# Modulation rows in units of 1024 by 512, in pairs, with a pair in each stage end

## What is computed

```python
def adaln(cond, w, b):                       # w is (2048, 6*2048) per layer
    m = jax.nn.silu(cond) @ w + b            # shift, scale, gate, twice
    return [m.reshape(n, 6, 1, D_MODEL)[:, j] for j in range(6)]

for l in range(2):
    sh1, sc1, g1, sh2, sc2, g2 = adaln(cond, w_ada[l], b_ada[l])
    h = rmsnorm(x, norm_g[l, 0]) * (1 + sc1) + sh1
    y = mixer(l, h)                          # 0: neighbourhood attention, 1: gated linear attention
    x = x + g1 * rmsnorm(y, norm_g[l, 1])
    h = rmsnorm(x, norm_g[l, 2]) * (1 + sc2) + sh2
    x = x + g2 * rmsnorm(square(relu(h @ w1[l])) @ w2[l], norm_g[l, 3])
```

## Time and profile before

| | us |
|---|---|
| runs | 2574.95, 2575.25, 2572.07 |
| median | 2574.95 |
| profiled execution, its time | 2574.7 |
| profiled execution, its span | 2572.9 |
| PE busy | 2508.4 (97%) |
| DVE busy | 1366.2 (53%) |
| ACT busy | 1052.7 (41%) |
| DMA, mean | 247 GB/s |

### The profile page before, as it was taken

The page is one execution under the profiler, slowest core; times in us unless marked ns, Lnnn a source line. Parts: engine busy times, 40 slices in busy tenths (PEclk is TensorE's granted clock), DMA queues, the critical chain, the costliest instruction groups (busy, mean ns, idle before and its releaser), DMA issues.

```text
span 2572.9 us, 37557 instructions
## 1 busy us (share of the span) xinstructions
PE 2508.4 (97%) x14850; PEld 2027.9 (79%) x14850; DVE 1366.2 (53%) x1496; ACT 1052.7 (41%) x1148; POOL 114.6 (4%) x164
## 2 busy tenths in 40 slices
PE   6899999989999999999999999999899999999998
PEld 3578888778878878878777877897787888888887
DVE  2244445475545536536555454564765464564665
ACT  3223344363334333423353365583533333343342
POOL 0020000000000000000000032200000000000000
PEclk8999999999999999999999999999999999999999
DMA  9988988958878878878787754559588555555554
GB/s 361 360 271 287 291 287 285 348 174 277 294 252 272 281 243 279 278 259 264 265 300 266 251 179 159 166 169 334 179 260 288 183 187 205 166 193 197 184 196 175
DMA packets 497463, 634.54 MB, mean 247 GB/s; under 512 B 12128, under 2 KB 378512, under 8 KB 496080
## 3 DMA queue, kind: packets, MB, share of 16 engines
q1 hardware_dynamic: 488672, 608.46, 70.9%
q0 software_dynamic: 6352, 23.31, 2.6%
q10 hardware_dynamic: 2336, 1.31, 0.2%
HBM read 623.90 MB, written 9.13 MB: 246 GB/s over the span
## 4 chain that ended last, share of the span: by engine, by line
PE 80%; DMA 10%; DVE 5%; ACT 3%; issue 1%; SPq 0%; POOL 0%; ACTq 0%; DVEq 0%
PE PS L1256 23%; PE PS L1257 12%; PE PS L1324 10%; PE PS L1326 10%; PE PS L1325 10%; PE PS L1283 4%; DVE WLO L1816 3%; ACT WHI L1560 2%; DMA RAW<-in_w_qkvg_gla 2%; DMA RAW<-in_w_o_na 2%; DMA RAW<-in_w_mlp 2%; DMA RAW<-in_w_o_gla 2%; PE PS L1265 2%; PE PS L1267 1%; PE PS L1266 1%; DMA SCR<-in_w_ada 1%
## 5 line engine op out<-in xcount | busy, mean ns | idle before, releaser
L1816 DVE TENSOR_TENSOR WLO<-RAW,WHI 128x2048 fp32r<-128x2048 f32 x384 | 878.8, 2300 | 767.0 <-ACT WHI L1560 762.2
L1560 ACT ACTIVATE WHI<-RAW 128x2048 fp32r<-128x2048 f32 x384 | 731.7, 1915 | 729.7 <-DMA RAW<-in_w_mlp 484.8
L1256 PE MATMUL PS<-HM,WHI 128*128 128x512 f32 x2560 | 913.8, 401 | 7.3 <-DVE SCR L2053 3.5
L1257 PE MATMUL PS<-HM,WLO 128*128 128x256 f32 x2560 | 718.5, 281 | 0.0
L1256 PEld LDWEIGHTS PS<-HM,WHI 128*128 128x128 f32 x2560 | 482.2, 188 | 139.3 <-issue 18.4
L1257 PEld LDWEIGHTS PS<-HM,WLO 128*128 128x128 f32 x2560 | 484.6, 189 | 0.2
L1324 PE MATMUL PS<-WHI,HID 128*128 128x512 f32 x1152 | 453.9, 394 | 6.0 <-DVE WLO L1816 6.0
L1325 PE MATMUL PS<-WLO,HID 128*128 128x512 f32 x1152 | 449.6, 390 | 0.0
L1326 PE MATMUL PS<-WHI,HID 128*128 128x512 f32 x1152 | 449.2, 390 | 0.0
L1324 PEld LDWEIGHTS PS<-WHI,HID 128*128 128x128 f32 x1152 | 216.8, 188 | 63.6 <-issue 19.3
L1326 PEld LDWEIGHTS PS<-WHI,HID 128*128 128x128 f32 x1152 | 216.8, 188 | 45.9
(11 more groups left out here) (238 smaller groups left out, 1882.4 us busy)
## 6 DMA issues: line engine op xcount, KB each, us to landing
RAW<-in_w_mlp SPq DMA_DIRECT2D x256, 1024.0 KB, 5.8
ADW<-in_w_ada SPq DMA_DIRECT2D x176, 1024.0 KB, 8.5
RAW<-in_w_qkv_na SPq DMA_DIRECT2D x48, 1024.0 KB, 6.8
RAW<-in_w_qkvg_gla SPq DMA_DIRECT2D x32, 1024.0 KB, 6.4
SCR<-in_w_ada SPq DMA_DIRECT2D x16, 1024.0 KB, 11.3
RAW<-in_w_o_na SPq DMA_DIRECT2D x16, 1024.0 KB, 7.1
RAW<-in_w_qkvg_gla SPq DMA_DIRECT2D x32, 512.0 KB, 4.8
RAW<-in_w_o_gla SPq DMA_DIRECT2D x16, 1024.0 KB, 7.0
```

The lines of the kernel that those rows point to most:

```text
L1256: mm(bank[:, 0:2 * T2], hi[:, k, cols], act[:, kc, 0:2 * T2], start=first, stop=False)
L1257: return mm(bank[:, 0:T2], lo[:, k, cols], act[:, kc, 0:T2], start=False, stop=last)
L1560: actv(WHI[:, 2 * s + u, 0:n], RAW[:, u, 0:n], ACT.Copy).then_inc(hi_done, 1)
L1816: tt(WLO[:, 2 * s + u, 0:n], RAW[:, u, 0:n], WHI[:, 2 * s + u, 0:n].bitcast(f32), ALU.subtract).then_inc(lo_done, 1)
```

## The change

- A unit is now 1024 rows by 512 columns, also 2 MB; its two halves are 512 rows by 512 columns. Two units (`odd` 0 and 1) accumulate in one bank, and give the same two rows of 256 as before. PE does 8 products of 512 columns per unit instead of 16 of 256. `row_ready` is waited for once in a pair.
- ACT copies and stores a pair as two halves of 256 columns, after both units. In attention this is at odd r, both halves in a row, each copy followed by its two stores, ahead of the split.
- There are 80 units as before. MLP 0 has 10 a group instead of 9, and the four stretches after it fewer.
- Each stage end has a pair instead of a single unit: the first unit ahead of the last turning of stream 0, the second behind it. ACT copies both after all four quarters of modulation.
- On SP the pair's loads take both places of the last output slab.

```diff
-        A_MLP0 = 5 * D // UC + 1
-        GU = 2 * NB + 1
-        A_QKV1 = A_MLP0 + HID_GROUPS * GU + 1
-        A_WO1 = A_QKV1 + NB + 2
-        A_MLP1 = A_WO1 + NB + 1
-        LU = 2 * NB - 1
-        A_END = A_MLP1 + LU
-        BETWEEN = {0: A_MLP0 - 1, 1: A_QKV1 - 1, 2: A_MLP1 - 1}
+        A_MLP0 = 5 * D // UC + 2
+        GU = 2 * NB + 2
+        A_QKV1 = A_MLP0 + HID_GROUPS * GU + 2
+        A_WO1 = A_QKV1 + NB
+        A_MLP1 = A_WO1 + NB
+        A_END = A_MLP1 + NB
+        BETWEEN = {0: A_MLP0 - 2, 1: A_QKV1 - 2, 2: A_MLP1 - 2}
...
-        PLAN_WO0, PLAN_WO, PLAN_V = ((0, 1), (2, 3), (4, 5), ()), ((0,), (1,), (2, 3), ()), ((0, 1), (2, 3), (4,), (5,))
-        PLAN_MLP = {GU: ((0,), (1,), (2, 3), (4,)), LU: ((0,), (1,), (2,), ())}
+        PLAN_WO0, PLAN_WO, PLAN_V = ((0, 1), (2, 3), (4, 5), ()), ((0,), (1,), (), ()), ((0,), (1,), (2,), (3,))
+        PLAN_MLP = {GU: ((0, 1), (2, 3), (4, 5), ()), NB: ((), (), (), ())}
...
                 if r == LAST:
-                    ada_row(A_QKV0 + r)
+                    row_half(A_QKV0 + r - 1, 0)
+                    row_half(A_QKV0 + r - 1, 1, MROW_NA)
                 for x in heads:
                     turned_keys(x)
-                if r < LAST:
-                    ada_row(A_QKV0 + r, r == 0)
+                if r < LAST and r % 2:
+                    row_half(A_QKV0 + r - 1, 0, first=r == 1)
+                    row_half(A_QKV0 + r - 1, 1, MROW_NA, first=r == 1)
                 split_hi(m, s, UNIT, (0,))
-                store_row(A_QKV0 + r)
...
-            def load_ada(a, layer, col):
+            def load_ada(a, layer, col, odd):
                 for u in range(2):
                     sp.wait_ge(ada0_used if u == 0 else ada_done, a + 1)
-                    src = w_ada[layer, u * UNIT_ROWS:(u + 1) * UNIT_ROWS, ds(col, UC)] \
-                        .rearrange("(c p) n -> p c n", p=P)
-                    sp.dma_start(ADW[:, u, :].rearrange("p (c n) -> p c n", c=UKC), src).then_inc(ada_in[u], 16)
+                    row = UNIT_ROWS * odd + YC * u
+                    src = w_ada[layer, row:row + YC, ds(col, AC)].rearrange("(c p) n -> p c n", p=P)
+                    sp.dma_start(ADW[:, u, :].rearrange("p (c n) -> p c n", c=4), src).then_inc(ada_in[u], 16)
...
             def with_between(plan, n):
-                return plan[n] + ((max(map(max, filter(None, plan))) + 1,) if n == YN - 1 else ())
+                last = max(map(max, filter(None, plan)))
+                return plan[n] + ((last + 1, last + 2) if n == YN - 1 else ())
...
-            def ada_rows(a, bank=ROWB):
-                pe.wait_ge(row_ready, a)
+            def ada_rows(a, odd, bank=ROWB):
+                if not odd:
+                    pe.wait_ge(row_ready, a)
                 for u in range(2):
                     pe.wait_ge(ada_in[u], ada_loads(a))
-                    w = ADW[:, u, :].rearrange("p (c n) -> p c n", c=UKC)
-                    for r in range(2):
-                        for j in range(4):
-                            k = 4 * r + j
-                            end = mm(bank[32 * j:32 * j + 32, 0:UC], CS[:, UKC * u + k, :], w[:, k, :],
-                                     start=(u == 0 and r == 0), stop=(u == 1 and r == 1))
+                    w = ADW[:, u, :].rearrange("p (c n) -> p c n", c=4)
+                    for j in range(4):
+                        end = mm(bank[32 * j:32 * j + 32, 0:AC], CS[:, UKC * odd + 4 * u + j, :], w[:, j, :],
+                                 start=(not odd and u == 0), stop=(odd == 1 and u == 1))
                     end.then_inc(ada0_used if u == 0 else ada_done, 1)
...
             def turn_rest(f, m0):
+                first = BETWEEN[f - 1]
+                pe.wait_ge(bank_free, evacuated(m0, YN - 2, 1))
+                ada_rows(first, 0, BETWEEN_ROWB)
                 turn_stream(f, 0, range(2, 4))
-                pe.wait_ge(bank_free, evacuated(m0, YN - 2, 1))
-                ada_rows(BETWEEN[f - 1], BETWEEN_ROWB)
+                ada_rows(first + 1, 1, BETWEEN_ROWB)
                 turn_stream(f, 1, range(4))
-                pe.wait_ge(row_ready, BETWEEN[f - 1] + 1)
+                pe.wait_ge(row_ready, first + 2)
...
-                    ada_row(BETWEEN[f], False, BETWEEN_ROWB)
                     modulate(f + 1, shift, 2)
-                    store_row(BETWEEN[f])
-                    modulated_hi(f + 1, 0)
                     modulate(f + 1, shift, 3)
-                    for g in range(1, 4):
+                    copy_half(BETWEEN[f], 0, MROW[:, :], BETWEEN_ROWB)
+                    copy_half(BETWEEN[f], 1, MROW_LATER, BETWEEN_ROWB)
+                    for g in range(4):
                         modulated_hi(f + 1, g)
+                    store_half(BETWEEN[f], 0, MROW[:, :])
+                    store_half(BETWEEN[f], 1, MROW_LATER)
```

More of the change, by code:

```diff
@@ L1298, in step @@
                             banks_read()
-                        ada_rows(ada)
-            def stream(m, bodies, body, ada, a=0, filled=None, start=0, banks_read=None):
-                with pe.Fori(start, bodies) as i:
-                    for s in range(2):
-                        step(i * 2 + (m + s), s, body, i * ada + (a + s) if s < ada else None, filled, banks_read)
+                        ada_rows(ada, odd)
             def filled(f):
@@ L1503, in mlp_group @@
             def mlp_group(g, layer, m, a, f, per, norm=None):
-                with pe.Fori(0, NB) as i:
-                    for s in range(2):
-                        slab = g * (4 * NB) + i * 2 + (m + s)
-                        ada = g * per + i + a if s == 0 and a is not None else None
-                        step(slab, s, features_out(HM), ada, filled(f), modulated(2 * layer + 1))
+                with pe.Fori(0, NB // 2) as pair:
+                    for x in range(2):
+                        for s in range(2):
+                            slab = g * (4 * NB) + pair * 4 + (m + 2 * x + s)
+                            ada = g * per + pair * 2 + (a + x) if s == 0 and a is not None else None
+                            step(slab, s, features_out(HM), ada, x, filled(f), modulated(2 * layer + 1))
                 for n in range(YN):
@@ L1587, in round_hidden, with step @@
                          ACT.Copy).then_inc(hid_hi, 1)
-            def step(m, s, ada=None, hidden=None, prefetch=True):
-                if prefetch:
-                    split_hi(m + 1, 1 - s)
-                if ada is not None:
-                    ada_row(ada)
-                if hidden is not None:
-                    round_hidden(*hidden)
-                if ada is not None:
-                    store_row(ada)
-            def stream(m, bodies, ada, a=0, start=0):
-                with act.Fori(start, bodies) as i:
-                    for s in range(2):
-                        step(i * 2 + (m + s), s, i * ada + (a + s) if s < ada else None)
+            def step(m, s, pair=None, hidden=None):
+                split_hi(m + 1, 1 - s)
+                if pair is not None:
+                    row_half(pair, s)
+                round_hidden(*hidden)
             def square(x, f, n, b):
@@ L1644, in out_slab @@
                     out_squares(m0, f, n - 1)
-                for a in ada[:1]:
-                    ada_row(a)
-                    store_row(a)
+                if pair is not None and not pair[1]:
+                    row_half(pair[0], 0)
                 if f is not None and n == YN - 1:
@@ L1764, in mlp @@
                 first = 1 if last else 0
-                per = LU if last else GU
+                per = NB if last else GU
                 if last:
@@ L1773, in mlp_group @@
             def mlp_group(g, layer, m, a, per, complete=False, last=False):
-                with act.Fori(0, NB) as i:
-                    for s in range(2):
-                        slab = g * (4 * NB) + i * 2 + (m + s)
-                        ada = g * per + i + a if s == 0 and a is not None else None
-                        step(slab, s, ada, (g * KC + i * 4 + (layer * HID_GROUPS * KC + 2 * s), i, s))
+                with act.Fori(0, NB // 2) as two:
+                    for x in range(2):
+                        for s in range(2):
+                            slab = g * (4 * NB) + two * 4 + (m + 2 * x + s)
+                            pair = g * per + two * 2 + a if x and a is not None else None
+                            step(slab, s, pair, (g * KC + two * 8 + (layer * HID_GROUPS * KC + 4 * x + 2 * s),
+                                                 two * 2 + x, s))
                 m0 = g * (4 * NB) + (m + 2 * NB)
```

113 lines of the change are left out of this document (62 added, 51 removed).

## The result

The changed kernel takes 2662.82 us, median of 4 runs (2656.97 to 2664.15), beside 2575.1 us (2572.07 to 2575.43) of the kernel before: 1.0339 times, interval 1.0321 to 1.0357, or 88 us more. It is slower, as forecast, and within the range of 2618 to 2668. It is 16 us above the 2647 that was named, and above the 2636 to 2658 that the prediction gave the forecast itself. The profiled execution has a span of 2662.0 us, 89.1 more than before.

What follows compares the result with a forecast made beforehand. TensorE, busy 97% of the span, was taken as the bound, so only added work or waits count. 2574.7 + 61 (ends) + 17 (attention) - 5 (fetch) = 2647.7, taken as 2647 us; range 2618 to 2668, its own 2636 to 2658.

Steps and rivals of the forecast that it cites:

- width: TensorE's modulation units: 8 products of 512 columns take the same time as 16 of 256; 0 taken, 1.6 us at most.
- ends: Three stage ends: late loads +19.4, half clock +3.0, unit moved in -2.1, so 20.3 us each; 61 us taken for three.
- attention: Odd slabs: ScalarE's copies and stores delay the split by 2.85 us; TensorE's waits sum to 17 us, bounds 4 and 22.
- MLP 0: Copies and stores lie beside TensorE's products: nothing, or up to 4 us if its loads come late.
- fetch and its half clock: Last slab before each end: 2 KB rows load faster; 3 us off waits, 2 off half clock, bounds 0 and 8.
- the three signs that were named: Stage ends: pieces issued 2.8 us after the first unit, ScalarE's DMA wait over 15 us, last product to first 30 us.
- The shift: First end: VectorE's sum for stream 1 comes at 570.5 instead of 551.03, 19.4 us later, delaying the next stage's first product.
- its second part: Stage ends: half clock in the first 5 us of the next stage, 1.5 us behind its first product.
- absorb the shift: Rival in attention: slack hides ScalarE's later split, so its 17 us go and the time is 2630 us; chance 0.13.
- Wide products were not cheaper: Rival on TensorE's units: wide products cost less per column, 37 us go, giving 2610 us; chance 0.04.
- That the pair is hidden: Rival in the ends: the next pieces reach ScalarE by 539.68, nothing moves; 2563 us if attention's cost is hidden; chance 0.03.
- The rival of dearer ends: Each end costs 24 us or so through less prefetch and longer half clock, with MLP 0's waits: 2665 us; chance 0.12.

Runs made afterwards that it cites:

- both runs: Kernel before, narrow units, a pair in each stage end: 2578.38 us; the same with the first slab of values emptied and one unit fewer in WO1's third: 2575.16 us.

## Why the prediction was right, and where it was off

The terms of its sum beside what they came to. The ends are counted with the 6.3 us of their three units that left other stages, MLP 0 without the 8.4 us of its four more; what the fetch saved is taken as the fall of WO0, values to WO1 and MLP 1 (19.4 us) over the seven units that the last two gave up (14.7).

| term | forecast | measured |
|---|---|---|
| width | 0 | 0 |
| ends | +61 | 59.1 - 6.3 = +52.8 |
| attention | +17 | +22.4 |
| MLP 0 | 0, bound 4 | +18.1 |
| fetch and its half clock | -5 | -4.7 |
| sum | +73 | +88.6 |

The direction and the mechanism of the largest term were right. That the time is only 16 us above the one named is in part luck: the ends came 8 us cheaper than forecast, against 5 us more in attention and 18 us in MLP 0 that no term had.

- **Direction and mechanism: right.** The row in which SP stood 21.0 us for a unit told that SP blocks at this wait; whatever is put behind it there comes late. Issue of the pieces 2.7 us after the unit's start (forecast 2.8), ScalarE's wait over 15 us (20.8), 30 us from last product to first (31.3, 29.7, 30.2): the three signs that were named are there at all three ends.
- **Ends: 8 us too much in all.** The shift was right: from TensorE's last product to VectorE's sum it was 2.7 us (548.33 to 551.03) and is 21.9 (569.14 to 590.99), 19.2 more where 19.4 was said; and from there to the next stage's first product it is 1.5 us longer (9.9 instead of 8.35), the half clock's first part. Wrong was its second part, 1.5 us behind the first product: in the first end the clock was at half there before too (3.4 us from 560.0, now 3.4 us from 601.2), and behind the first product of the other two it is full in both kernels, so 4.5 us were counted that cost nothing. Most of the rest is that the second and third end grew by 1.2 and 1.8 us less than the first, from which all three were reckoned.
- **Attention: 5 us too little.** The waits were forecast as 16.8 us and are 16.1: seven of some 1.0, six of some 0.8, 2.43 at slab 1 and 1.90 at the last. The step that failed is that the sum took waits alone: those of 2.43 and 1.90 us each brought 3.4 us at half clock (195.0 and 447.6), which costs 3.4 us together, and the sum had half clock only in the ends. The other 2.9 us are likely TensorE's refilling behind 15 waits, which was counted for a unit (0.2 us) and not here; no run separates it.
- **MLP 0: the term that was mis-sized.** "Copies and stores there lie beside TensorE's products" was true, and not the question. Of the 18.1 us, 7.1 are the jump stalls and 1.7 the half clock behind them, 2.8 the last group's waits for a unit, 2.0 the longer wait at 1393 (3.79 us, where 1.79 were before), and 3.4 the 6.8 us at half clock behind it; 1.1 are spread. The jump's part is shown by the runs; the last group's is read from its rows, and no run put its units elsewhere. Nothing in the trace of before showed a stall at a jump, since its code was not fetched again; but the change's own code makes TensorE's group longer (by 141 records), and that was not weighed. The upper bound of 4 us had the last group's cause and not its half clock.
- **Rivals.** Attention did not absorb the shift. Wide products were not cheaper. That the pair is hidden failed on the loads, and not for want of time in the end: with the right order and bank it is hidden, and still wins nothing that can be measured: in both runs longer waits for late loads stand elsewhere, ahead of the third end above all. The rival of dearer ends, 2665, came nearest in size, but not by its mechanism: the ends were cheaper than forecast, and the terms that it names (3.7 us more for each end, 4 us for MLP 0) make 15 us and not its 18.

## What to carry to other kernels

Before work is moved into a gap, look at which queue brings its data and what stands behind the wait there: a loading queue that blocks on one buffer turns a gap of 11 us into 30. Beside the work that an edit moves, look at how long it makes the body of a loop on the busiest engine. Give a wait on TensorE the half clock that can follow it: in the changed kernel 3.4 us at the lower level, which cost 1.7, followed waits of 1.90, 2.43 and 3.08 us, and 6.8 us followed one of 3.79; none followed the one of 2.87. Where loads and products are as nearly balanced as here, a unit hidden in one place can come back as a wait elsewhere, as it did in both plans that were run.

## What was not expected of the hardware

- A loop body of 1461 records on TensorE ran its second and third pass with no packet on its instruction queue in 392 us; bodies of 1602 and 1796 fetched 8 or 9 packets of 16.4 KB a pass, and TensorE stood 1.9 to 3.2 us at each jump back.
- Halving the number of modulation products and their weight loads, at twice the width, changed nothing: TensorE's busy time in them is 155.6 against 154.9 us.
- ScalarE begins no operation while it issues, though one that it has begun goes on (the split of 1.91 us runs while the stores are issued). A pair of small stores (1.16 and 1.13 us) left it idle for 1.31 and 1.26 us; that was 22 us of the time when they stood ahead of a split, and nothing behind it.
